# Hybrid attention, delta-rule and mixture-of-experts block on one core: a seventh place for gate and up weights, and a quarter of the leading weights' low part moved to VectorE

## What is computed

```python
def reference(x, mem, ...):
    h = rmsnorm(x, norm_mix_g[l])
    x = x + parallel_mixers(h, ...)
    h = rmsnorm(x, norm_x_g[l])
    m = rmsnorm(mem, norm_mem_g[l])
    x = x + memory_cross_attention(h, m, ...)
    h = rmsnorm(x, norm_ffn_g[l])
    x = x + hierarchical_moe(h, ...)
    return rmsnorm(x, norm_final_g)

def hierarchical_moe(h, ...):
    ...
    for e in range(N_EXPERTS):
        hid = jax.nn.silu(t @ w_exp_gate[e]) * (t @ w_exp_up[e])
        out = out + combine[:, e:e + 1] * (hid @ w_exp_down[e]).astype(jnp.float32)
```

## Time and profile before

| | us |
|---|---|
| Median of three executions | 829.1 |
| The profiled execution: its own time | 829.2 |
| Its span, first to last instruction | 827.4 |
| TensorE busy | 775.1 (94%) |
| VectorE busy | 343.8 (42%) |
| GpSimd busy | 312.3 (38%) |
| ScalarE busy | 239.2 (29%) |
| Mean granted TensorE clock, of full speed | 0.994 |

### The profile page before, as it was taken

The page is one execution under the profiler, slowest core; times in us unless marked ns, Lnnn a source line. Parts: engine busy times, 40 slices in busy tenths (PEclk is TensorE's granted clock), DMA queues, the critical chain, the costliest instruction groups (busy, mean ns, idle before and its releaser), DMA issues.

```text
span 827.4 us, 14485 instructions
## 1 busy us (share of the span) xinstructions
PE 775.1 (94%) x5739; PEld 623.0 (75%) x5739; DVE 343.8 (42%) x767; ACT 239.2 (29%) x417; POOL 312.3 (38%) x354
## 2 busy tenths in 40 slices
PE   5999999999999999999999999998999999988785
PEld 5987788888988877788888887866777777756651
DVE  6466651474575484325512624372222221121126
ACT  5344242112221458632222445331111111110012
POOL 3774434542242244143542454334333333322111
PEclk9999999999999999999999999999999999999998
DMA  9956832402202232446478255679999999999976
GB/s 250 167 108 119 266 66 55 98 2 52 51 1 53 51 102 52 94 102 187 81 157 229 70 173 183 254 282 343 388 388 388 390 387 383 392 386 381 390 299 250
DMA packets 74347, 166.95 MB, mean 202 GB/s; under 512 B 18838, under 2 KB 46310, under 8 KB 66344
## 3 DMA queue, kind: packets, MB, share of 16 engines
q1 hardware_dynamic: 65856, 150.66, 57.7%
q0 software_dynamic: 5392, 9.61, 3.5%
q10 hardware_dynamic: 3032, 5.74, 2.2%
HBM read 157.31 MB, written 16.97 MB: 211 GB/s over the span
## 4 chain that ended last, share of the span: by engine, by line
PE 64%; DMA 25%; DVE 4%; POOL 2%; issue 2%; ACT 2%; SPq 1%; DVEq 0%; POOLq 0%; ACTq 0%
DMA arena<-in_w_exp_up 23%; PE bank L1067 15%; PE bank L1074 13%; PE bank L1076 13%; PE bank L1075 13%; PE bank L1424 2%; DMA arena<-y_half 1%; PE bank L1434 1%; PE bank L1115 1%; PE bank L1225 1%; PE bank L1167 1%; POOL w_low L889 1%; PE bank L1279 1%; POOL xres L927 1%; PE bank L1411 1%
## 5 line engine op out<-in xcount | busy, mean ns | idle before, releaser
L869 POOL TENSOR_TENSOR ring_low<-ring,w_high 128x512 fp32r<-128x512 f32 (+1 forms) x64 | 83.6, 1306 | 124.7 <-ACT w_high L1516 120.7
L1074 PE MATMUL bank<-h_hi,w_high 128*128 128x512 f32 x296 | 122.1, 412 | 0.9 <-ACT arena L1630 0.9
L1075 PE MATMUL bank<-h_lo,w_high 128*128 128x512 f32 x296 | 115.8, 391 | 0.0
L1424 PEld LDWEIGHTS bank<-arena,hT 128*64 128x64 f32 x1728 | 96.6, 136 | 24.1 <-issue 12.5
L1424 PE MATMUL bank<-arena,hT 128*64 128x128 f32 x1728 | 100.7, 274 | 8.2 <-DMA arena<-in_w_exp_up 6.1
L869 POOL TENSOR_TENSOR w_low<-ring,w_high 128x512 fp32r<-128x512 f32 x56 | 75.1, 1341 | 59.9 <-ACT w_high L1516 55.8
L2142 DVE SCALAR_TENSOR_TENSOR rt<-rt,bank 128x128 f32<-128x128 f32 x32 | 9.2, 288 | 175.2 <-ACT rt L1733 175.2
L1516 ACT ACTIVATE w_high<-ring 128x2048 fp32r<-128x2048 f32 (+1 forms) x32 | 58.9, 1839 | 57.1 <-PE bank L1076 37.2
L1074 PEld LDWEIGHTS bank<-h_hi,w_high 128*128 128x128 f32 x296 | 55.7, 188 | 15.2 <-issue 3.5
L1076 PE MATMUL bank<-h_hi,ring_low 128*128 128x512 f32 x168 | 66.1, 393 | 0.0
L1075 PEld LDWEIGHTS bank<-h_lo,w_high 128*128 128x128 f32 x296 | 55.7, 188 | 9.5
(11 more groups left out here) (325 smaller groups left out, 1368.7 us busy)
## 6 DMA issues: line engine op xcount, KB each, us to landing
arena<-in_w_exp_gate SPq DMA_DIRECT2D x27, 1024.0 KB
arena<-in_w_exp_up SPq DMA_DIRECT2D x27, 1024.0 KB
arena<-in_w_exp_down SPq DMA_DIRECT2D x27, 1024.0 KB
ring<-in_w_in SPq DMA_DIRECT2D x33, 512.0 KB, 6.7
ring<-in_w_exp_gate SPq DMA_DIRECT2D x5, 1024.0 KB
ring<-in_w_exp_up SPq DMA_DIRECT2D x5, 1024.0 KB
ring<-in_w_exp_down SPq DMA_DIRECT2D x5, 1024.0 KB
xres<-in_x SPq DMA_DIRECT2D x8, 512.0 KB, 7.3
```

The source lines that it names most:

```text
L869: after(pool.tensor_tensor(low, full, high, ALU.subtract), w_lo if kk == KD - 2 else step["pool"])
L1074: pe.matmul(o, l_hi, r_hi, start=(n == 0), stop=False)
L1075: pe.matmul(o, l_hi, r_lo, start=False, stop=False)
L1424: ins = pe.matmul(bank[CAP * half:CAP * half + CAP, 1, P * n:P * n + P], xgT[:, x, kk, :], w[:, kk, P * half:P * half + P], start=(kk == 0 ...
```

## The change

It has four parts.

1. Gate and up weights get seven places instead of six (`GATES = 7`), down weights keep six. Place seven is the last 2048 words of `arena` for gate, and the residual rows of tiles 2 and 3 in `xres` for up. Expert 6's gate weights are issued right behind the three loads of expert 4, and its up weights after `xres` has been read. From expert 7 on, the queue's order is gate and up of e, then down of e - 1; the last two loads are down of 30 and down of 31. The places of the half-results at the end (`y_rows`) move with it, and the final gains are loaded after `down_done` 29.
2. So that `xres` is free, the residual rows of tile 3 go into accumulators (banks 2 and 3) before the experts: two new jobs `("k3", 0)` and `("k3", 1)` behind `("g0", 3)`, and `keep_residual` is gone from the loop. Job `ls` moves to bank 5.
3. The cross-attention's low part goes to the rows of `hT` instead of `h_lo` (`out_lo`), so that the up weights of expert 3 are issued with its gate and down weights.
4. Of the leading weights' low part, GpSimd takes three quarters and VectorE the fourth, behind its copy of tile 1's second half, with a semaphore of its own, `lead_lo`.

```diff
-KEEP_AT = {26: 3}
+GATES = UNROLL + 1
...
-    jobs += [("g0", 0), ("g0", 1), ("pos", 3), ("g0", 2), ("g0", 3), ("ls",), ("gt",), ("most",)]
+    jobs += [("g0", 0), ("g0", 1), ("pos", 3), ("g0", 2), ("g0", 3), ("k3", 0), ("k3", 1), ("ls",), ("gt",), ("most",)]
...
-LATE_BANKS = {"g0": 0, "gt": 0, "ls": 3, "most": 4, "kr": 6}
+LATE_BANKS = {"g0": 0, "gt": 0, "k3": 2, "ls": 5, "most": 4, "kr": 6}
+KEPT = ("kr", "k3")
...
+        x_row_parts = y_hi[:, :, :].rearrange("p k t -> p (k t)")
+        out_lo = [x_row_parts[:, D * t + 512:D * t + D].rearrange("p (k l) -> p k l", k=4) for t in range(NT)]
...
             if c in part_of and not low_in_place(c):
                 eng.wait_ge(w_lo, part_of[c] + 1)
+                if part_of[c] == 0:
+                    eng.wait_ge(lead_lo, 1)
...
-            first = 2 * EW + (2 * t + j) * D
+            first = (UNROLL - 2) * EW - 2 * D + (2 * t + j) * D
...
+        def expert_parts(e):
+            def home(b):
+                return arena[:, b * EW:(b + 1) * EW] if b < UNROLL - 1 else ring[:, :, :].rearrange("p r w -> p (r w)")
+            n = e % GATES
+            if n < UNROLL:
+                gate, up = home(n)[:, 0:KD * FE], home(n)[:, KD * FE:2 * KD * FE]
+            else:
+                gate, up = arena[:, arena_words - KD * FE:arena_words], xres[:, 2:NT, :].rearrange("p t d -> p (t d)")
+            return [gate.rearrange("p (k f) -> p k f", k=KD), up.rearrange("p (k f) -> p k f", k=KD),
+                    home(e % UNROLL)[:, 2 * KD * FE:EW].rearrange("p (k n) -> p k n", k=2)]
...
             job_done(sp, ("cq", X_HEADS - 1))
-            load_part(3, 0)
-            load_part(3, 2)
+            for i in range(3):
+                load_part(3, i)
...
-            load_part(3, 1)
             sp.wait_ge(hrow_ready, NT)
             for i in range(3):
                 load_part(4, i)
...
-            def load_expert(i, b):
-                parts, sources = expert_parts(b), expert_sources(i * UNROLL + b)
-                sp.wait_ge(w_loaded[(b - 2) % UNROLL], i * 32 + (32 if b >= 2 else 0))
+            def load_gate(e):
+                sp.dma_start(expert_parts(e)[0], expert_sources(e)[0]).then_inc(w_loaded[e % UNROLL], 16)
+            def load_up(e):
+                sp.dma_start(expert_parts(e)[1], expert_sources(e)[1]).then_inc(w_loaded[e % UNROLL], 16)
+            def load_down(e):
+                sp.wait_ge(down_done, e + 1 - UNROLL)
+                sp.dma_start(expert_parts(e)[2], expert_sources(e)[2]).then_inc(down_loaded[e % UNROLL], 16)
+            load_gate(GATES - 1)
+            job_done(sp, ("k3", 1))
+            load_up(GATES - 1)
+            for e in range(GATES, EXPERTS):
+                sp.wait_ge(w_loaded[(e - 2) % UNROLL], 32 * ((e - 2) // UNROLL) + 32)
                 sp.sem_inc(loading, 1)
-                sp.wait_ge(gu_done, i * UNROLL + (b + 1 - UNROLL))
-                for n in range(2):
-                    sp.dma_start(parts[n], sources[n]).then_inc(w_loaded[b], 16)
-                sp.wait_ge(down_done, i * UNROLL + (b + 1 - UNROLL))
-                sp.dma_start(parts[2], sources[2]).then_inc(down_loaded[b], 16)
-            for i in range(1, TURNS):
-                for b in range(UNROLL):
-                    load_expert(i, b)
-            for b in range(REST):
-                load_expert(TURNS, b)
+                sp.wait_ge(gu_done, e + 1 - GATES)
+                load_gate(e)
+                load_up(e)
+                load_down(e - 1)
+            load_down(LAST_EXPERT)
...
+            sp.wait_ge(down_done, EXPERTS - 3)
             sp.dma_start(gain_out, norm_final_g.rearrange("(o d) -> o d", o=1).to_broadcast([P, D])).then_inc(gains_in, 16)
-            sp.wait_ge(down_done, EXPERTS - 4)
...
-            for n in range(4):
-                s = slice(n * CHUNK_W // 4, (n + 1) * CHUNK_W // 4)
+            for n in range(3):
+                s = lead_quarter(n)
                 pool.wait_ge((lead_hi, w_hi)[n // 2], 1)
-                after(pool.tensor_tensor(w_low[:, 0, s], lead[:, s], w_high[:, 0, s].bitcast(F32), ALU.subtract), w_lo if n == 3 else step["pool"])
+                after(pool.tensor_tensor(w_low[:, 0, s], lead[:, s], w_high[:, 0, s].bitcast(F32), ALU.subtract), w_lo if n == 2 else step["pool"])
...
+                                pe.wait_ge(lead_lo, 1)
...
-                if k == "kr":
-                    job_empty(pe, ("co", 2, job[1]))
-                    return pe.matmul(o, ident, xres[:, 2, 512 * job[1]:512 * job[1] + 512], start=True, stop=False, skip_group_check=True)
+                if k in KEPT:
+                    t = 2 + KEPT.index(k)
+                    job_empty(pe, ("co", t, job[1]))
+                    return pe.matmul(o, ident, xres[:, t, 512 * job[1]:512 * job[1] + 512], start=True, stop=False, skip_group_check=True)
...
-                gate, up, _ = expert_parts(b)
+            def gate_up(e, x, s):
+                gate, up, _ = expert_parts(e)
...
-                if e1 in KEEP_AT:
-                    keep_residual(KEEP_AT[e1])
-            def keep_residual(t):
-                for half in range(2):
-                    pe.matmul(sum_banks(t)[:, half, :], ident, xres[:, t, 512 * half:512 * half + 512], start=True, stop=False, skip_group_check=True)
...
+                        if (phase, t, q) == ("mix", 1, 1):
+                            dve.wait_ge(w_hi, 1)
+                            s = lead_quarter(3)
+                            after(tt(w_low[:, 0, s], chunk(split_chunks[0])[:, s], w_high[:, 0, s].bitcast(F32), ALU.subtract), lead_lo)
...
-                    after(tt(h_lo[s], oh4, h_hi[s].bitcast(F32), ALU.subtract), e)
+                    after(tt(out_lo[c], oh4, h_hi[s].bitcast(F32), ALU.subtract), e)
```

22 lines of the change are left out of this document (10 added, 12 removed).

## The result

The change takes **831.85 us** (median of 7 runs, 831.14 to 832.69), the kernel before on the same chip 829.19 (828.96 to 830.45): a ratio of 1.0032, with an interval from 1.0023 to 1.0041. It is slower by 2.7 us, and the forecast's range ended at 831.2. In a second measurement the ratio was 1.0042 (1.0029 to 1.0056). The profiled execution took 832.35 us, its span is 830.4.

What follows compares the result with a forecast made beforehand. The prediction took the bound to be when the expert-weight stream becomes continuous, the bytes then left, and the work after the last bytes. Terms 0 - 2.1 + 0 + 2.6 - 0.6 = -0.1 gave 829.1 us, range 826.9 to 831.2.

Steps and rivals of the forecast that it cites:

- Part 1: Leading weights, VectorE taking GpSimd's fourth quarter: `("z", 0, 1)` starts where it did, 0 us, between -0.2 and +1.3.
- Rival (a): At the beginning, TensorE's clock halves after a 2 us pause, slowing `("z", 0, 1)`: +1.7, 830.8 us; chance 0.28.
- Part 2: Expert 3's up weights issued earlier: queues run dry 2.4 us near 551, so of 2.5 us moved 0.1 is gained.
- Part 3: Seventh place closes the stream's hole at 562 to 565: 2.0 us, -2.1 with expert 3's earlier up weights; bounds -1.1, -2.8.
- Part 4: Identity matmuls before the experts start the loop 2.2 us later, hidden by TensorE's store of weights: cost 0.
- that cover of 1.2 us: Queues stay busy until about 568 with expert 6's 2 MiB and gathers, while expert 7's data comes at 566.8.
- Part 5: Load order at the end: expert 30's down matmuls start at 797.56 instead of 794.94, +2.6; scatter gives back 0.6.
- the scatter's gain: Expert 30's scatter, 4.1 us beside weights, would run after them: -0.6, between 0 and -1.2.
- The signs that I named: Expected in the change's profile: moved TensorE waits, closed hole, empty windows near 551, later first expert, times of the last experts.
- (c): Stream runs dry again as expert 7 waits for late TensorE, or VectorE's chain isn't relieved: +1.3, 830.4 us; chance 0.10.
- the forecast's gain: At the stream's start, seventh place together with expert 3's earlier up weights: -2.1 us.

Runs made afterwards that it cites:

- the second profile: Profile from the second measurement of the kernel before with only expert 30's down weights moved behind gate and up of 31: 1.0034 (1.0021 to 1.0046), +2.8 us.

## Why the prediction was wrong

- **What bounds the kernel** was read rightly (the stream's start, and what follows the last bytes), but one line was missing: a pause of TensorE costs more than its length where the clock falls behind it. I gave that a place at the beginning only.
- **Part 1, 0 us.** The time was right, `("z", 0, 1)` at 26.97 for 26.8, behind 2.2 us of pause, but by luck. I had it wait for VectorE until 26.8, and VectorE was done at 25.69; GpSimd, whose low parts I had left out, was done at 26.83. Nor did `("z", 0, 1)` wait for VectorE before: TensorE was still busy then. Rival (a) happened, in some executions: +1.1 us by the part alone (0.25 to 1.8), and +0.2 once the pause was filled. I argued against it with waits of up to 1.6 us in the loop at a clock of 1.00. I had read the waits for `arena` alone (the ring has one of 1.95 us, at full clock too), and all of those stand between two dense groups.
- **Part 2, -0.1:** 1.0000 alone, which agrees; a gain so small can't be measured here.
- **Part 3, -2.1:** right where it was reckoned. At 566 us the change is 2.1 us ahead. It was not kept.
- **Part 4, "Cost 0, if that cover of 1.2 us holds": this step failed.** I counted the 2.2 us of the identity matmuls and left out the wait for the gather of expert 1, of which I had only counted the bytes. It had travelled in the hole; the seventh place filled the hole, its first packet moved 4.3 us after the issue instead of 1.8, and the rows came 2.3 us too late for TensorE, with the fall behind it. Expert 8's loads left at 579.96, which is 7.5 us after 572.47 and not the 2.2 that I had added. Filling that one pause gave back 1.5 us, starting the experts earlier 1.6; the intervals of these ratios overlap a little with the change's, so the sizes are rough.
- **Part 5, +2.6 and -0.6.** The place was right (797.31 for 797.56, alone), the scatter's gain was too small: 1.6 us, at 2.5 instead of 4.1. The sum of 2.0 is what the second profile shows at the loads of the half-results, by chance: the scatter's gain, 1.0 us larger than mine, stands against 1.25 us lost to the clock, which I hadn't. The medians say 2.8 and 3.9, and what they have beyond 2.0 is open. Nor was the order a matter of the last pair alone, as I had it: in all late experts it costs 2.4 us with six places, and the old order there gives 2 to 3 us back with seven, while in the change moving back the last pair alone gave nothing.
- **The signs that I named:** the waits at 19 and 27 us, the hole, the empty windows near 551 and the first expert at 561.4 (561.55) came as written; expert 30's down matmuls at 795.5 (799.23) and the half-results at 802.3 (805.06) did not.
- **The slow rivals** were right in kind and each too small: (a) 830.8 and (c) 830.4. (c) named the right symptom, a stream that runs dry because of expert 7, with too small a cause; it was expert 8. I took them as alternatives; the second profile of the change has both together.

Added up, the parts measured alone in the kernel before and the forecast's gain give 1.1 + 1.7 + 2.4 - 2.1 = 3.1 us, between the 2.7 and 3.5 that the change measured. With about 1 us of uncertainty on each, this shows only that no large term is missing.

## To carry to other kernels

When loads are reordered, ask of each wait not only how long it is but what it stands next to: waits between two dense groups of matmuls mostly kept the clock here (4 falls in 56), waits among short pauses lost it far more often (16 in 30), also where they were no longer. When a hole in the stream is filled, list what travelled in it unnoticed (here a gather on another queue) and who waits for that. And where TensorE must pause, some thrown-away matmuls can be worth more than they cost: 2.0 us of them, inside a wait of 2.3, gave about 1.5 us back.

## What the runs showed of the hardware

- **Falls of the clock behind short pauses.** The granted clock went from 1.00 to 0.50 (2.4 to 1.2 GHz) in or behind waits of 2.2 us at the beginning, 1.7 to 2.3 us at the gather and 1.0 to 2.8 us before down matmuls (3.10 in the last pair), seldom behind one of 2.0 to 2.2 us between two experts, and was down for 3.4 us in most cases, for 6.8 us in some and once for 10.2. The same wait in two executions of one kernel had a fall once and none the other time: the 2.21 us at the beginning of the change. So a single profile of such a kernel isn't its median; the spread of the runs is part of the result.
- **What such a fall costs.** Eight down matmuls took 3.2 to 3.7 us instead of 1.94. The Trainium skill (TensorE: Matmul & The Clock Gate, HAM oscillation) describes a loop in which a wait for DMA in every tile brings the clock down anew, and charges half of the time spent at the low clock. On the half the trace agrees: eight down matmuls at 0.50 lose 1.25 to 1.75 of their 3.2 to 3.7 us. The waits of that loop are of about 3 to 5 us; here waits of 1.0 to 2.8 us had falls too. Of the loss not all reaches the end: in the kernel before with the change's late order, three falls take 5.1 us of the granted clock (half of three stretches of 3.4), and this execution took 829.95 us, 1.3 more than the kernel before; the change with the gather's wait filled lost as much in its late experts and took 828.90.
- **A gather beside a full queue.** The first indirect DMA of 64 rows on GpSimd's queue took 9.5 us from issue to use beside weights at 431 GB/s. With the hole in the stream the rows were used without a wait 6.2 us after the issue. Over all gathers whose landing the traces show, the median from issue to landing is 7.2 us in the kernel before and 7.4 in the change. The scatter of expert 30 took 4.1 us beside weights and 2.5 after them.
